# Differential attention head loop: moved taps, diagonals, rotary copies, values and layer norm's root

## The chip, the cores and the metric

One core of a Trainium2 chip runs the whole program. The metric is the device time in microseconds (us) of that core. TensorE does the matmuls, VectorE, ScalarE and GpSimd work on tiles of 128 partitions, and the sync engine's queue issues the weights' DMAs. Each engine runs its own list of instructions in order, and waits on semaphores for the others.

## The reference, cut to what matters

The program computes two transformer blocks over 512 tokens of width 1024 in float32. The change lies in the mixer of the second block, which joins differential attention with a convolution:

```python
def hybrid_mixer(h, positions, ...):
    q, k, v, u = split(h @ w_in)                 # 4 heads; q and k have 2 components of 64, v has 128
    q, k = partial_rope(q), partial_rope(k)
    # causal; for each head and component:
    p = softmax(q @ k.T / sqrt(64))
    a = p[0] - lam * p[1]                        # lam is one scalar
    a = rmsnorm(a @ v, subln_g) * (1 - lam_init) # over a head's 128 values
    c = u[..., :512] * sigmoid(u[..., 512:])
    c = causal_dwconv(c, cv_dw_w) + cv_dw_b      # 31 taps
    c = silu(layernorm(c, cv_ln_g, cv_ln_b))
    return concat(a, c) @ w_out
```

Cross attention over 256 memory rows follows, and its keys and values (`m @ w_ckv`) don't depend on the mixer, so they are computed in between.

## The kernel before, in words

Activations are held feature by feature: a tile is 128 features by 512 tokens. To keep float32 accuracy in matmuls, each operand is split into a high part (suffix `H`, written by ScalarE's copy) and a low part (suffix `L`, what remains, made by VectorE's `low`), and a product takes three matmuls (`three`, L468 to L470). Weights come in pieces of 128 x 512: a DMA to one of 4 `raw` buffers, then a split by GpSimd (L2557, L2559) to one of 7 slots, which comes free when TensorE has used the piece.

All order is written out by hand, once for each engine: the functions `pe`, `act`, `dve`, `pool` and `sync` hold the same named steps, each in its own engine's order, and `wait_ge(engine, event)` and `did(event)` connect them. There is no planner. PSUM has eight banks. `take` pops the first bank of a list and waits until its last reader is done, and `give` puts it at the end with the event that frees it. Two banks are kept out of this queue for a time: that of the convolution by VectorE (`acc_bank`) and that of the convolution tile by TensorE (`ctap`).

The steps of the stage, for four heads `hd`, each with two projections `j = 2 hd` (q) and `2 hd + 1` (k):

- `rotary_in(j)`: TensorE projects to the bank `rt`; ScalarE copies it to `tmp[j % 2]`.
- `rotate(j)`: TensorE permutes `tmp` (L961) to the bank `rts`; VectorE multiplies by cosine and sine and adds; ScalarE makes the high half of q or k; `rotated(j)` on VectorE makes the low half (`d_qL`, `d_kL`).
- `d_scores(hd)`: for each of four query tiles `n`, TensorE makes the scores of both components (L978), and adds the mask (L981). VectorE takes the maximum (L2359), ScalarE the exponential and its sum, VectorE the inverse, and ScalarE and VectorE combine the two components in `d_P`. `between` holds work that TensorE does behind a tile.
- `d_turned(hd)`: TensorE transposes the probabilities in four tiles (L1007), split to `uH`/`uL` rows 4 to 7.
- `d_values(hd)`: values by probabilities into the bank `do`, which ScalarE squares into `sums`.
- `stat_end("dn", hd)`: TensorE sums the squares over features with a matrix of ones (L501); ScalarE's `rstd` makes the root (logarithm, then exponential); `d_normed` scales the tile and splits it.
- Convolution: of 4 tiles, VectorE does three, 31 taps each (`some_taps`), TensorE the fourth by diagonal matrices (`conv_taps`, L996) that ScalarE makes (`diagonals`), eight buffers in rotation. `convolved(i)` is ScalarE's copy out of the bank.
- Layer norm: `mu` sums four tiles (L1051), VectorE centres (`cent`), squares are summed, `stat_end("ln")` and `rstd("ln")` give the root, VectorE scales (`lnn`), ScalarE applies silu.
- `memory_keys(4)`, `memory_keys(6)` and `xvalues(0)` are the memory's keys and values; the output projection `w_out_2` opens with three output tiles at once (`three_open`, `three_step`).

Of the kernel before, what the change touches and what calls it, by code (L numbers as in the profile page):

```python
# [279 lines left out]
BY_PE = 3  # L280


def build(nc, xT, pT, memT, pos, pos2, vec, cst, ws, out):
    PLAN, BEHIND, DIVIDED = plan()
    with ExitStack() as ctx:
# [147 lines left out]
        def pe():  # L433
# [3 lines left out]
            def take(*event):  # L437

                b = banks.pop(0)
                if b.freed:  # L440
                    P.wait_ge(*b.freed)
                bank_of[event] = b.ap
                return b
# [514 lines left out]
            def rotate(j):  # L958
                b = take("rts", j)
# [51 lines left out]
            def d_values(hd):  # L1011
# [9 lines left out]
                give(b, V, "y2L", hd)  # L1021
# [17 lines left out]
            for hd in range(2):  # L1039
# [4 lines left out]
                rotate(2 * hd + 5)  # L1044
                conv_taps(20 + 8 * hd, min(24 + 8 * hd, 31))
                d_values(hd)
                stat_end("dn", hd, tiles=1, tail=False)
            b = take("mu")
# [6 lines left out]
            d_turned(2)  # L1055
            d_scores(3, {1: lambda: memory_keys(4)})
            memory_keys(6)
            stat_end("ln", tiles=4, tail=False, freed=(V, "lnn", 3))
            d_values(2)
            stat_end("dn", 2, tiles=1, tail=False)  # L1060
            d_turned(3)
            xvalues(0)
            d_values(3)
            stat_end("dn", 3, tiles=1, tail=False)
# [6 lines left out]
            for k in (0, 1, 2, 4, 5, 6, 7, 3):  # L1071
                three_step(lin, k, uH, uL, y2_ready, last=3)
            three_give(lin, *[(V, "h wo", o) for o in range(3)])
# [108 lines left out]
        def root(*sid):  # L1182

            if sid[0] in ("mix", "mlp", "ple", "hs", "cq", "ckv", "ln"):
                return bk("stat", *sid)[:, :]
            return tab[1][0][:, 0:256] if sid == ("mem",) else rs[:, :]
# [3 lines left out]
        def act():  # L1190
# [397 lines left out]
            def rotary_in(j):  # L1588
                A.wait_ge(P, "rt", j)
                if j > 1:  # L1590
# [9 lines left out]
            def d_scores(hd):  # L1600
# [5 lines left out]
                for n in range(4):  # L1606
# [9 lines left out]
                    if n:  # L1616
                        divide(n - 1)
                divide(3)
# [13 lines left out]
            def d_normed(hd):  # L1632
                A.wait_ge(V, "dn", hd)
                do(uH[:, hd, :], bk("do", hd)[:, :], ACT.Copy).then_inc(*A.did("y2H", hd))
# [23 lines left out]
            d_scores(0)  # L1658
            diagonals(12, 16)
            rotary_in(2)  # L1660
# [4 lines left out]
            for hd in range(2):  # L1665
                d_turned(hd)
                d_scores(hd + 1)
                diagonals(20 + 8 * hd, 28 + 8 * hd)
                rotary_in(2 * hd + 4)
                rotary_in(2 * hd + 5)  # L1670
                rotate(2 * hd + 4)
                rotate(2 * hd + 5)
                d_values(hd)
                rstd(128, "dn", hd)
                d_normed(hd)
            convolved(2)
            for i in range(4):
                A.wait_ge(V, "cent", i)
                square(("ln",), i, d_acc[:, i, :])
            d_turned(2)  # L1680
            d_scores(3)
            memory_keys(4)
            memory_keys(6)
            rstd(512, "ln")
            d_values(2)
            rstd(128, "dn", 2)
            d_normed(2)
            d_turned(3)
# [102 lines left out]
        def dve():  # L1791
# [529 lines left out]

            def rotate(j):
                t, y = tmp[j % 2][:, :], bk("rt", j)[:, :]
                s = 1.0 if j % 2 else 0.125
                V.wait_ge(A, "rt", j)
                V.wait_ge(V, "turn")
                stt(y, y, s, C[:, :], MUL, MUL).then_inc(*V.did("rc", j))
                V.wait_ge(P, "rts", j)
                stt(t, bk("rts", j)[:, :], s, Sn[:, :], MUL, MUL).then_inc(*V.did("rts", j))
                V.wait_ge(V, "rts", j)  # L2330
                tt(y, y, t, ADD).then_inc(*V.did("rr", j))
# [7 lines left out]
            def d_scores(hd):  # L2339
# [12 lines left out]
                for n in range(4):  # L2352
# [9 lines left out]
                    if n:  # L2362
                        combine(n - 1)
                combine(3)
# [24 lines left out]

            rotate(0)  # L2390
            rotate(1)
# [4 lines left out]
            d_scores(0)  # L2396
            some_taps(2)
            rotate(2)
            rotate(3)
            rotated(2)  # L2400
            some_taps(1)
            rotated(3)
            for hd in range(2):
# [290 lines left out]
```

## Time and profile before

| | |
|---|---|
| median of 3 runs | 2405.92 us (2403.82 to 2407.05) |
| the profiled execution | 2401.89 us, span 2400.0 us |
| TensorE busy | 2298.3 us, 96% of the span |
| VectorE, ScalarE, GpSimd busy | 53%, 27%, 65% |
| mean granted clock of TensorE | 0.988 |

The profile is of one execution. The span runs from its first to its last instruction, and the profiled execution's own time, 2401.89 us, contains it. Times of a row are measured from the span's start. The stage of this change lies between about 1689 and 1850 us.

### The profile page before, as it was taken

How to read it: one execution, taken by the hardware profiler on the slowest of the kernel's cores; microseconds unless marked ns; L12 is line 12 of the kernel's file. 1: busy time of each engine (PE TensorE's matmuls, PEld its weight loads, DVE VectorE, ACT ScalarE, POOL GpSimd, SP SyncE). 2: the span in 40 equal slices, each digit the busy share in tenths (PEclk: the TensorE clock that was granted, in tenths of full speed). 3: DMA queues.
4: the chain of work that ended last, by engine and by line, in shares of the span. 5: the costliest groups of instructions: out<-in, count | busy, mean ns of one | idle time of the engine just before them, and what ended most of it. 6: DMA issues, size and time to landing. Idle time of an engine off the chain costs nothing.

```text
span 2400.0 us, 27442 instructions
## 1 busy us (share of the span) xinstructions
PE 2298.3 (96%) x10372; PEld 1860.2 (78%) x10372; DVE 1269.0 (53%) x1820; ACT 648.8 (27%) x1190; POOL 1563.6 (65%) x1530
## 2 busy tenths in 40 slices
PE   8999989999998899999999999999988999999998
PEld 6888877888887577778778888778647787888886
DVE  6674726235346666165454364468763443635444
ACT  3443432101014355154221011141444232202112
POOL 7556557877775454554597777598315946878784
PEclk9999999999999899999999999999998999999999
DMA  5222222333332111211233333233112422333332
GB/s 163 77 71 82 68 80 83 107 99 98 97 92 75 53 39 37 70 40 45 75 117 105 99 110 101 79 101 106 48 31 71 113 63 79 97 98 96 99 95 75
DMA packets 110867, 200.13 MB, mean 83 GB/s; under 512 B 12304, under 2 KB 18704, under 8 KB 110736
## 3 DMA queue, kind: packets, MB, share of 16 engines
q1 hardware_dynamic: 107568, 194.72, 27.0%
q10 hardware_dynamic: 3168, 3.67, 0.5%
q8 instruction: 82, 1.34, 0.2%
q14 instruction: 49, 0.40, 0.0%
HBM read 196.24 MB, written 2.10 MB: 83 GB/s over the span
## 4 chain that ended last, share of the span: by engine, by line
PE 87%; DVE 7%; ACT 2%; POOL 2%; issue 1%; DMA 0%; SPq 0%; DVEq 0%; POOLq 0%; ACTq 0%
PE bank L468 26%; PE bank L470 26%; PE bank L469 26%; DVE bank L1801 2%; DVE h L1793 1%; POOL wL L2559 1%; PE bank L501 1%; PE bank L996 1%; POOL wH L2557 1%; PE bank L862 1%; PE bank L867 1%; PE bank L868 1%; PE bank L863 1%; PE bank L864 1%; DVE aL L1801 1%
## 5 line engine op out<-in xcount | busy, mean ns | idle before, releaser
L2559 POOL TENSOR_TENSOR wL<-raw,wH 128x512 fp32r<-128x512 f32 (+2 forms) x731 | 997.9, 1365 | 60.9
L2557 POOL TENSOR_SCALAR wH<-raw 128x512 fp32r<-128x512 f32 (+2 forms) x731 | 528.9, 724 | 650.3 <-PE bank L470 558.4
L468 PE MATMUL bank<-aH,wH 128*128 128x512 f32 x1376 | 546.1, 397 | 18.1 <-DVE aL L1801 8.8
L470 PE MATMUL bank<-aH,wL 128*128 128x512 f32 x1376 | 537.6, 391 | 0.0
L469 PE MATMUL bank<-aL,wH 128*128 128x512 f32 x1376 | 537.1, 390 | 0.0
L468 PE MATMUL bank<-uH,wH 128*128 128x512 f32 x960 | 375.5, 391 | 5.6 <-DVE uL L1793 5.6
L469 PE MATMUL bank<-uL,wH 128*128 128x512 f32 x960 | 374.4, 390 | 0.0
L470 PE MATMUL bank<-uH,wL 128*128 128x512 f32 x960 | 374.3, 390 | 0.0
L468 PEld LDWEIGHTS bank<-aH,wH 128*128 128x128 f32 x1376 | 258.8, 188 | 77.8 <-issue 12.4
L469 PEld LDWEIGHTS bank<-aL,wH 128*128 128x128 f32 x1376 | 259.0, 188 | 56.3 <-issue 3.7
L470 PEld LDWEIGHTS bank<-aH,wL 128*128 128x128 f32 x1376 | 258.7, 188 | 54.9
L468 PEld LDWEIGHTS bank<-uH,wH 128*128 128x128 f32 x960 | 180.8, 188 | 44.6 <-ACT uH L1205 6.4
L469 PEld LDWEIGHTS bank<-uL,wH 128*128 128x128 f32 x960 | 180.8, 188 | 37.9 <-issue 0.5
L470 PEld LDWEIGHTS bank<-uH,wL 128*128 128x128 f32 x960 | 180.7, 188 | 37.8
L1205 ACT ACTIVATE uH<-mr 128x512 fp32r<-128x512 f32 x64 | 40.5, 633 | 391.0 <-DVE mr L1801 391.0
L1793 DVE TENSOR_TENSOR F<-F,bank 128x512 f32<-128x512 f32 x56 | 38.5, 687 | 190.0 <-PE bank L470 190.0
L1801 DVE SCALAR_TENSOR_TENSOR mr<-bank,rs 128x512 f32<-128x512 f32 x64 | 44.0, 688 | 157.9 <-PE bank L470 142.0
L1801 DVE SCALAR_TENSOR_TENSOR bank<-F,vs,bank 128x512 f32<-128x512 f32 x138 | 103.8, 752 | 34.9 <-ACT bank L1205 23.8
L1793 DVE TENSOR_TENSOR h<-h,bank 128x512 f32<-128x512 f32 x88 | 60.4, 686 | 112.4 <-PE bank L470 110.8
L1793 DVE TENSOR_TENSOR sums<-sums,sq 128x512 f32<-128x512 f32 (+1 forms) x72 | 78.3, 1088 | 76.5 <-ACT sq L1205 76.4
L2566 POOL TENSOR_SCALAR m_P<-m_P,m_stat 128x512 f32<-128x512 f32 x64 | 44.7, 698 | 102.0 <-DVE m_stat L2217 100.0
L1801 DVE SCALAR_TENSOR_TENSOR c_cb<-c_xb,vs,c_cb 128x511 f32<-128x511 f32 x88 | 82.4, 937 | 40.3 <-ACT c_cb L1205 38.7
(306 smaller groups left out, 3209.7 us busy)
## 6 DMA issues: line engine op xcount, KB each, us to landing
raw<-in_ws SPq DMA_DIRECT2D x699, 256.0 KB, 2.6
raw<-in_ws SPq DMA_DIRECT2D x24, 192.0 KB, 2.3
h<-in_xT SPq DMA_DIRECT2D x4, 512.0 KB, 6.6
E<-in_memT ACTq DMA_DIRECT2D x16, 128.0 KB, 2.5
out<-c_F SPq DMA_DIRECT2D x8, 256.0 KB, 2.1
tmp<-in_pT ACTq DMA_DIRECT2D x4, 256.0 KB, 3.6
raw<-in_ws SPq DMA_DIRECT2D x8, 128.0 KB, 2.0
g_hc<-in_cst SPq DMA_DIRECT2D x1, 640.0 KB, 9.2
```

Source lines behind the costliest of these rows:

```text
L468: P.e.matmul(o, lH, rH, start=start, stop=False, skip_group_check=skip)
L469: P.e.matmul(o, lH, rL, start=False, stop=False, skip_group_check=skip)
L470: return P.e.matmul(o, lL, rH, start=False, stop=stop, skip_group_check=skip)
L501: i = P.e.matmul(b.ap[:, 0:n], ones, sums[:, 0:n], start=True, stop=not tail)
L862: P.e.matmul(b.ap[:, :], m_qnH[:, c], m_knH[:, :], start=True, stop=False)
L863: P.e.matmul(b.ap[:, :], m_qnH[:, c], m_knL[:, :], start=False, stop=False)
L1205: return A.e.activation(o, i, func, bias=bias, scale=scale)
L1793: return V.e.tensor_tensor(o, a, b, op)
L1801: return V.e.scalar_tensor_tensor(o, a, s, b, op0, op1)
L2557: G.e.tensor_scalar(H, x, 1.0, 0.0, MUL, ADD).then_inc(*G.did("wH", n))
L2559: G.e.tensor_tensor(L, x, H.bitcast(F32), SUB).then_inc(*G.did("w", n))
L2566: G.e.tensor_scalar(x, x, m_st[:, 4 * (hd % 2) + n, 2:3], 0.0, MUL, ADD).then_inc(*G.did("mP", hd, n))
```

## The change

In the order of the engines:

- TensorE: `take` may take the second bank of the queue. In the head loop `d_values(hd)` moves between the two rotations, the second of which takes the second bank; three taps stand between it and the statistic, and in the first pass one behind it. The `do` bank is freed by the normed tile (`dn`). `d_turned(2)` goes ahead of `mu`; the layer norm's statistic reads `sq` and its bank is freed by ScalarE's logarithm; `d_turned(3)` goes ahead of the statistic of head 2, and the statistic of head 3 behind the first step of the output projection.
- ScalarE: `d_scores` gets `between` too: diagonals and the first rotary copy go between query tiles 2 and 3, the third convolved tile too; the transposed probabilities go ahead of `d_normed`; the layer norm's squares go to four buffers in head 3's scores.
- VectorE: the product with cosine gets its own step (`turned_by_cos`); taps go between query tiles; the normed tile is written to `tmp[0]` instead of its bank; the layer norm's root is in the SBUF tile `C`; its squares are added by `add_ln_squares` in head 3's scores.

```diff
@@ pe: take, rotate, d_values, head loop
-            def take(*event):
-                b = banks.pop(0)
+            def take(*event, second=False):
+                b = banks.pop(1 if second else 0)
...
-            def rotate(j):
-                b = take("rts", j)
+            def rotate(j, second=False):
+                b = take("rts", j, second=second)
...
-                give(b, V, "y2L", hd)
+                give(b, V, "dn", hd)
...
                 rotary_in(2 * hd + 5)
                 rotate(2 * hd + 4)
-                rotate(2 * hd + 5)
-                conv_taps(20 + 8 * hd, min(24 + 8 * hd, 31))
                 d_values(hd)
+                rotate(2 * hd + 5, second=True)
+                conv_taps(20 + 8 * hd, 23 + 8 * hd)
                 stat_end("dn", hd, tiles=1, tail=False)
+                if hd == 0:
+                    conv_taps(23, 24)
+            d_turned(2)
             b = take("mu")
...
-            d_turned(2)
             d_scores(3, {1: lambda: memory_keys(4)})
             memory_keys(6)
-            stat_end("ln", tiles=4, tail=False, freed=(V, "lnn", 3))
+            b = take("stat", "ln")
+            P.wait_ge(V, "sum", ("ln",))
+            P.e.matmul(b.ap[:, :], ones, sq[:, :], start=True, stop=True).then_inc(*P.did("stat", "ln"))
+            give(b, A, "ln", "ln")
             d_values(2)
+            d_turned(3)
             stat_end("dn", 2, tiles=1, tail=False)
-            d_turned(3)
             xvalues(0)
             d_values(3)
-            stat_end("dn", 3, tiles=1, tail=False)
...
                 three_step(lin, k, uH, uL, y2_ready, last=3)
+                if k == 0:
+                    stat_end("dn", 3, tiles=1, tail=False)
@@ root
-            return tab[1][0][:, 0:256] if sid == ("mem",) else rs[:, :]
+            return tab[1][0][:, 0:256] if sid == ("mem",) else C[:, :] if sid == ("ln",) else rs[:, :]
@@ act
-                if j > 1:
+                if j in (4, 6):
+                    A.wait_ge(V, *(("y2L", 0) if j == 6 else ("rr", 2)))
+                elif j > 1:
                     A.wait_ge(V, "rr", j - 2)
...
-            d_scores(0)
-            diagonals(12, 16)
-            rotary_in(2)
+            d_scores(0, {2: lambda: (diagonals(12, 16), rotary_in(2))})
...
-                d_turned(hd)
-                d_scores(hd + 1)
-                diagonals(20 + 8 * hd, 28 + 8 * hd)
-                rotary_in(2 * hd + 4)
+                if hd == 0:
+                    d_turned(0)
+                d_scores(hd + 1, {2: lambda: (convolved(2) if hd else None, diagonals(20 + 8 * hd, 28 + 8 * hd), rotary_in(2 * hd + 4))})
                 rotary_in(2 * hd + 5)
                 rotate(2 * hd + 4)
+                d_values(hd)
                 rotate(2 * hd + 5)
-                d_values(hd)
                 rstd(128, "dn", hd)
+                d_turned(hd + 1)
                 d_normed(hd)
-            convolved(2)
-            for i in range(4):
-                A.wait_ge(V, "cent", i)
-                square(("ln",), i, d_acc[:, i, :])
-            d_turned(2)
-            d_scores(3)
+            def squares():
+                for i, x in enumerate((sq, tmp[1], C, Sn)):
+                    A.wait_ge(V, "cent", i)
+                    do(x[:, :], d_acc[:, i, :], ACT.Square).then_inc(*A.did("sq", ("ln",), i))
+            d_scores(3, {1: squares})
...
+            d_values(2)
             rstd(512, "ln")
-            d_values(2)
+            d_turned(3)
             rstd(128, "dn", 2)
             d_normed(2)
-            d_turned(3)
@@ dve
+            def turned_by_cos(j):
+                y = bk("rt", j)[:, :]
+                V.wait_ge(A, "rt", j)
+                V.wait_ge(V, "turn")
+                stt(y, y, 1.0 if j % 2 else 0.125, C[:, :], MUL, MUL).then_inc(*V.did("rc", j))
...
             def d_normed(hd):
-                y = bk("do", hd)[:, :]
+                y = tmp[0][:, :]
                 V.wait_ge(A, "rstd", "dn", hd)
-                stt(y, y, lam[:, 5:6], root("dn", hd), MUL, MUL).then_inc(*V.did("dn", hd))
+                V.wait_ge(V, *(("rr", 2 * hd + 4) if hd < 2 else ("y2L", hd - 1)))
+                stt(y, bk("do", hd)[:, :], lam[:, 5:6], root("dn", hd), MUL, MUL).then_inc(*V.did("dn", hd))
...
-                d_turned(hd)
-                d_scores(hd + 1)
-                some_taps(6)
+                d_scores(hd + 1, {2: lambda: some_taps(4)} if hd == 0 else {1: lambda: some_taps(200)})
+                turned_by_cos(2 * hd + 4)
+                some_taps(1)
                 rotate(2 * hd + 4)
+                turned_by_cos(2 * hd + 5)
+                rotated(2 * hd + 4)
                 rotate(2 * hd + 5)
-                rotated(2 * hd + 4)
-                some_taps(1)
                 rotated(2 * hd + 5)
+                if hd:
+                    V.wait_ge(P, "ctap")
+                    ts(d_acc[:, BY_PE, :], bk("ctap")[:, :], vv("cv_dw_b_2", BY_PE), None, ADD, None).then_inc(*V.did("conv", BY_PE))
                 d_normed(hd)
+                d_turned(hd + 1)
...
-            for i in range(1, 4):
-                add_squares(("ln",), i)
-            d_turned(2)
-            d_scores(3)
+            def add_ln_squares():
+                x = (sq, tmp[1], C, Sn)
+                for i in (0, 2):
+                    V.wait_ge(A, "sq", ("ln",), i + 1)
+                    tt(x[i][:, :], x[i][:, :], x[i + 1][:, :], ADD).then_inc(*V.did("sum2", ("ln",), i))
+                V.wait_ge(V, "sum2", ("ln",), 2)
+                tt(sq[:, :], sq[:, :], C[:, :], ADD).then_inc(*V.did("sum", ("ln",)))
+            d_scores(3, {1: add_ln_squares})
             memory_keys(4)
             memory_keys(6)
-            d_normed(2)
...
             d_turned(3)
+            d_normed(2)
```

## Rows read from the trace of the kernel before

**Rows 1.** Table by stretch: span, busy us (x instructions), clock, DMA, GB/s.

```profile
core 0: us, PE busy (x) PEld busy (x) DVE busy (x) ACT busy (x) POOL busy (x), PEclk, DMA share, GB/s
1689.40:1850.00 160.60, 139.22 (x620) 95.06 (x619) 93.34 (x187) 69.97 (x171) 55.72 (x59) 0.95 0.16 48
...
1762.20:1765.50 3.30, 3.30 (x6) 1.23 (x5) 2.97 (x8) 1.86 (x8) 0.00 (x0) 0.50 0.02 5
1799.70:1806.40 6.70, 4.36 (x20) 4.36 (x21) 4.37 (x13) 3.95 (x14) 1.18 (x2) 0.50 0.00 1
1827.00:1833.70 6.70, 4.84 (x12) 3.82 (x13) 3.36 (x7) 3.52 (x5) 1.69 (x2) 0.50 0.01 2
```

**Rows 2.** Waits of TensorE, 1683 to 1850: total us, times, longest.

```profile
PE bank L978 <- DVE uL L1793: 3.3, 3, 2.6
...
PE bank L501 <- ACT sums L1205: 2.9, 4, 0.8
PE bank L961 <- ACT tmp L1205: 2.3, 3, 1.7
PE bank L468 <- DVE d_qL L1793: 2.2, 2, 1.6
PE bank L1051 <- ACT F L1205: 1.6, 1, 1.6
```

**Rows 3.** Timeline of TensorE: start, us, instruction, [idle before <-releaser].

```profile
1745.46 1.96 PE L961 MATMUL bank<-tmp,cs 128*128 128x512 f32 x4 [1.67 <-ACT tmp L1205]
1747.26 3.60 PE L996 MATMUL bank<-F,sq 128*128 128x512 f32 x8
1752.46 0.50 PE L468 MATMUL bank<-uH,d_VH 128*128 128x512 f32 x1 [1.61 <-DVE d_qL L1793]
...
1755.27 1.13 PE L501 MATMUL bank<-sums,cs 128*128 128x512 f32 x2 [0.69 <-ACT sums L1205]
...
1756.23 1.25 PE L1007 MATMUL bank<-cs,F 128*128 128x128 f32 x10
1760.06 0.33 PE L978 MATMUL bank<-d_kH,d_qH 64*128 64x128 f32 x2 [2.57 <-DVE uL L1793]
...
1761.21 0.39 PE L978 MATMUL bank<-d_kH,d_qH 64*128 64x256 f32 x2 [0.23 <-DVE uL L1793]
...
1762.04 5.34 PE L996 MATMUL bank<-F 128*128 128x512 f32 x8
...
1802.04 0.58 PE L468 MATMUL bank<-x_mH,wH 128*128 128x256 f32 x1 [3.05 <-DVE uL L1793]
...
1809.85 0.45 PE L978 MATMUL bank<-d_kH,d_qH 64*128 64x384 f32 x2
...
1828.86 0.77 PE L468 MATMUL bank<-wH,x_mH 128*128 128x512 f32 x1 [5.24 <-DVE F L1801]
...
1845.19 1.10 PE L501 MATMUL bank<-sums,cs 128*128 128x512 f32 x2 [0.78 <-ACT sums L1205]
```

**Rows 4.** Timeline of ScalarE, same columns.

```profile
1744.74 1.06 ACT L1205 ACTIVATE tmp<-bank 128x512 f32<-128x512 f32 x2
...
1758.61 1.75 ACT L1205 ACTIVATE uH<-bank 128x512 fp32r<-128x512 f32 x4 [0.83 <-DVE bank L1801]
```

**Rows 5.** Timeline of VectorE, same columns.

```profile
1738.21 1.29 DVE L2359 TENSOR_REDUCE d_stat<-bank 128x1 f32<-128x512 f32 x2 [3.71 <-PE bank L981]
...
1757.82 0.76 DVE L1801 SCALAR_TENSOR_TENSOR bank<-bank,lam,rs 128x512 f32<-128x512 f32 x1 [4.16 <-ACT rs L1205]
...
1845.59 2.09 DVE L1793 TENSOR_TENSOR uL<-F,uH 128x512 fp32r<-128x512 f32 x2 [15.24 <-ACT uH L1205]
...
1850.59 0.69 DVE L1793 TENSOR_TENSOR uL<-bank,uH 128x512 fp32r<-128x512 f32 x1 [0.84 <-ACT uH L1205]
```

**Rows 6.** Timeline of GpSimd, same columns: one weight piece and the next's start.

```profile
1807.29 0.62 POOL L2557 TENSOR_SCALAR wH<-raw 128x512 fp32r<-128x512 f32 x1 [0.16 <-PE bank L470]
1807.99 1.29 POOL L2559 TENSOR_TENSOR wL<-raw,wH 128x512 fp32r<-128x512 f32 x1
1809.24 0.62 POOL L2557 TENSOR_SCALAR wH<-raw 128x512 fp32r<-128x512 f32 x1
```

More of the change, by code:

```diff
@@ L1182, in root @@
         def root(*sid):
-            if sid[0] in ("mix", "mlp", "ple", "hs", "cq", "ckv", "ln"):
+            if sid[0] in ("mix", "mlp", "ple", "hs", "cq", "ckv"):
                 return bk("stat", *sid)[:, :]
-            return tab[1][0][:, 0:256] if sid == ("mem",) else rs[:, :]
+            return tab[1][0][:, 0:256] if sid == ("mem",) else C[:, :] if sid == ("ln",) else rs[:, :]
         def act():
@@ L1598, in rotate, with d_scores @@
                 do(d_qk[2 * (j % 2)][:, :], bk("rt", j)[:, :], ACT.Copy).then_inc(*A.did("rH", j))
-            def d_scores(hd):
+            def d_scores(hd, between={}):
                 def divide(n):
@@ L1617, in d_scores @@
                         divide(n - 1)
+                    if n in between:
+                        between[n]()
                 divide(3)
@@ L1633, in d_normed @@
                 A.wait_ge(V, "dn", hd)
-                do(uH[:, hd, :], bk("do", hd)[:, :], ACT.Copy).then_inc(*A.did("y2H", hd))
+                do(uH[:, hd, :], tmp[0][:, :], ACT.Copy).then_inc(*A.did("y2H", hd))
             def convolved(i):
@@ L2324, in rotate @@
                 s = 1.0 if j % 2 else 0.125
-                V.wait_ge(A, "rt", j)
-                V.wait_ge(V, "turn")
-                stt(y, y, s, C[:, :], MUL, MUL).then_inc(*V.did("rc", j))
                 V.wait_ge(P, "rts", j)
@@ L2330, in rotate @@
                 V.wait_ge(V, "rts", j)
+                V.wait_ge(V, "rc", j)
                 tt(y, y, t, ADD).then_inc(*V.did("rr", j))
@@ L2337, in rotated, with d_scores @@
                 low(L[:, :], bk("rt", j)[:, :], H[:, :]).then_inc(*V.did("rL", j))
-            def d_scores(hd):
+            def d_scores(hd, between={}):
                 def combine(n):
@@ L2363, in d_scores @@
                         combine(n - 1)
+                    if n in between:
+                        between[n]()
                 combine(3)
@@ L2388, in xvalues @@
                     low(d_VL[:, 2 * t + half, :], bk("xV", half, t)[:, :], d_VH[:, 2 * t + half, :]).then_inc(*V.did("xVL", half, t))
+            turned_by_cos(0)
             rotate(0)
+            turned_by_cos(1)
             rotate(1)
@@ L2395, in dve @@
             some_taps(3)
-            d_scores(0)
-            some_taps(2)
+            d_scores(0, {2: lambda: some_taps(4)})
+            turned_by_cos(2)
             rotate(2)
+            turned_by_cos(3)
             rotate(3)
             rotated(2)
-            some_taps(1)
             rotated(3)
+            d_turned(0)
             for hd in range(2):
-                d_turned(hd)
-                d_scores(hd + 1)
-                some_taps(6)
+                d_scores(hd + 1, {2: lambda: some_taps(4)} if hd == 0 else {1: lambda: some_taps(200)})
+                turned_by_cos(2 * hd + 4)
+                some_taps(1)
                 rotate(2 * hd + 4)
+                turned_by_cos(2 * hd + 5)
+                rotated(2 * hd + 4)
                 rotate(2 * hd + 5)
-                rotated(2 * hd + 4)
-                some_taps(1)
                 rotated(2 * hd + 5)
+                if hd:
+                    V.wait_ge(P, "ctap")
+                    ts(d_acc[:, BY_PE, :], bk("ctap")[:, :], vv("cv_dw_b_2", BY_PE), None, ADD, None).then_inc(*V.did("conv", BY_PE))
                 d_normed(hd)
-            some_taps(200)
-            V.wait_ge(P, "ctap")
-            ts(d_acc[:, BY_PE, :], bk("ctap")[:, :], vv("cv_dw_b_2", BY_PE), None, ADD, None).then_inc(*V.did("conv", BY_PE))
+                d_turned(hd + 1)
             V.wait_ge(P, "mu")
```

## The prediction, made blind

> **What bounds the kernel now.** I began with the page's first part: TensorE is busy for 96% of the span (table above), so only its idle or slowed time can be won. The table by stretch then gives the total for the diff's stage: from 1689.4 to 1850.0 it is busy 139.22 of 160.60 us, so 21.4 us are idle, and three stretches have its granted clock at 0.50, the lower of its levels (1.2 GHz) [rows 1]. The waits of that window show for whom it stands: VectorE and ScalarE, never the weights [rows 2]. The timelines show each gap and the engines that end it [rows 3 to 6].
>
> A low clock costs only while there is work. Behind the gap of 1760 eight tap matmuls took 5.34 us instead of 3.60 [rows 3]: 1.7 us lost. In the second stretch work begins at 1802.04 and the low clock ends near 1806.4: half of 4.4, 2.2 us. In the third it is half of 1828.86 to 1833.8, 2.5 us. Together 6.4 us. All three stretches come with a gap of 2.57, 3.05 or 5.24 us [rows 1, 3]; smaller gaps had none. The Trainium skill (TensorE: Matmul & The Clock Gate, Part 1) says that the throttled state is the default and activity releases it; the rows agree.
>
> **What costs nothing.** The diff adds no matmul and leaves the weights' order and DMAs alone. TensorE's work in the stage is therefore constant, and the sum is idle and low clock before, less what is left of both.
>
> **Part 1: taps, diagonals and the first rotary copy between score tiles 2 and 3.** Before, ScalarE copies the first rotary tile behind the head's scores and eight diagonals, at 1744.74 [rows 4]; the rotation at 1745.46 had waited 1.67 us [rows 3]. Now the copy follows its projection, about 1737. Queued behind this wait on ScalarE are tile 3's exponentials; they need maxima of scores that come later still, at 1738.21, so nobody waits. VectorE idles for 3.71 us until then [rows 5]; four taps at about 0.75, 3.0 us, go into it (3.0 us more if that cover were gone). The waits at the rotations, L961, 2.3 us in three [rows 2], go.
>
> **Part 2: values between two rotations.** VectorE's chain of products, sum and low half behind the rotations kept the values waiting, 2.2 us in two heads [rows 2], because their bank was the one that the low half of q frees. Now they take a bank that a score tile freed long before, and the rotation behind them takes the second in the queue, free too. Squaring the values, which kept the statistic waiting 0.69 us [rows 3], lies under the rotation and three taps, 0.9 + 2.7 us (two matmuls of 0.45 to a tap, from 3.60 for eight [rows 3]). Both go in both heads.
>
> **Part 3: normed tile in SBUF, and the stalls that come.** Call S the start of a head's statistic. Before, S is 1755.27, the normed tile is done at 1758.58 (S + 3.31) and ScalarE turns to its high half at 1758.61; the next head's second score tile starts at 1761.21 (S + 5.94) [rows 3 to 5]. Counting banks in queue order, the fourth transposed tile now waits for the values' bank, free at S + 3.31. In the loop's first pass TensorE has before it the statistic 0.96, a tap 0.90 and nine of ten transposes, 1.12 (1.25 for ten [rows 3]): S + 3.0, a wait of 0.4. ScalarE now takes the probabilities' high halves first and starts that of the normed tile near S + 4.0, 0.65 later; on VectorE the probabilities' low halves are queued behind the normed tile's, and the second score tile waits for two of them, to S + 6.6. Between, TensorE has one score tile, 0.92 us (1761.21 - 0.23 - 1760.06 [rows 3]): it stands 2.1 us. I keep the 1.7 us of low clock here, for this is the place and kind of the gap that brought it before. In the second pass no tap stands behind the statistic: the fourth transposed tile waits from S + 2.1 to S + 3.4, 1.3 us; then the mean's eight matmuls, 3.6 us, reach beyond S + 6.6. The wait at head 1's second score tile stays, 0.5 us (what L978's 3.3 us leave beside 2.57 and 0.23 [rows 2, 3]).
>
> **Part 4: layer norm.** Its third convolved tile is copied during head 2's scores, so the mean no longer waits: L1051, 1.6 us [rows 2]. Centring, some 2.5 us of VectorE, used to stand before the low halves for which the memory keys waited 3.05 us at 1802.04 [rows 3]; those are now done ahead. Two score tiles 1.8, the keys 5.6 (1802.04 to 1809.85 less 2.2 [rows 3]) and tile 2, 1.1, put its scores some 5.9 us behind the centring's end. Exponentials, four squares at 0.6 and one addition end 5.4 to 6.5 us behind it. A lateness of 0.6 there has about 1 us of room before the last head's transposes need the last probability tile. I take 0; the bound is 1 us of waiting.
>
> **Part 5: root in SBUF, last heads.** Before, the statistic's bank came free with the fourth scaled tile, and the memory values waited 5.24 us for it at 1828.86 [rows 3]. Now it is free when ScalarE has read it, ahead of the transposes' end. The last two statistics go behind transposes and behind the first output step, so their part of L501's 2.9 us in four waits [rows 2] goes like that of the first two. The last probabilities are needed only behind the memory values, 11 us (1828.86 to 1844.4, less 2.5 of low clock and 2 of values [rows 3]).
>
> A price comes with it: a subtraction with both inputs in SBUF took 1.05 us (2.09 for two) beside GpSimd's work, one that read a bank 0.69 [rows 5]. Three low halves, four scalings and an addition become such: 8 x 0.4 = 3.2 us of VectorE. They lie under the memory values, but for those of the first passes, when GpSimd rests. I take 0 on the path, 3.2 as the bound. The Trainium skill (SBUF — State Buffer, Who interferes with whom) says that such an instruction contends with GpSimd's reads and that the first to start blocks the other. The 1.05 us agrees; by the rule the gain is at most 3.2 us less, and GpSimd loses as much.
>
> **Weights.** A piece costs GpSimd 0.62 + 1.29, by its starts 1.97 us [rows 6]; keys and memory values use one in 1.4 (5.6 for four). Seven lie ready when the keys start, at T. A slot is free again when its piece was used, so the last memory-value piece is ready 3.4 us behind the first one's use and needed 9.6 behind it; the first output piece at 5.4, needed at 12.7. No wait.
>
> **The sum.** Idle 21.4, low clock 6.4. A gap is counted from a modelled end that overlaps the next start (the statistic ends at 1756.40, the next matmul starts at 1756.23 [rows 3]), so each of twelve gaps gives another 0.16: 1.9. Left: 0.5 + 0.4 + 2.1 + 1.3 idle and 1.7 low clock, 6.0. Gain 21.4 + 6.4 + 1.9 - 6.0 = **23.7 us**. Work behind 1850 is TensorE's own and follows. The profiled execution took 2401.89 us (span 2400.0): it becomes 2378.2. The runs' median lies 4.0 above it, so **2382 us**. Bounds: no low clock, 1.7 more gain; the waits of 1 us and 3.2 us on the path and one more low stretch of 1.7, 5.9 less. Own range 2380 to 2388.
>
> **Rivals.**
> - *The chain moves rather than goes.* My 2.1 and 1.3 us come from the new orders on ScalarE and VectorE; further ones may. If both bring a second low stretch (2 x 1.7), the last transposes wait 2 us with another (3.7) and SBUF operands cost 3.2, the gain is 23.7 - 10.3 = 13.4: 2392.5. Against it: most covers exceed 1 us. Chance 0.17.
> - *No low clock and shorter new stalls.* The wait of 2.1 halves, low clock goes: 23.7 + 2.8: 2379. Chance 0.2.
> - *No change.* If taps overran their 3.71 us by several, each maximum, exponential and rotation in three heads would follow late, and 3 x 7 us would be back: 2403. The rows give a 3.0 us load. Chance 0.04.
> - *Slower.* Earlier demand finds GpSimd late. Fifteen pieces behind the seven are needed by T + 37; to lose 29 us there, past the gain and 5 more, 1.4 + 15c must exceed 66, so c over 4.3 us instead of 1.97. At 4.5 it is 1.4 + 67.5 - 37 = 32 us late: 2414. Contention adds under 1 us a piece. Chance 0.03.
>
> The forecast itself has 0.56. About 0.2% (5 us) is what a measurement of this kernel can tell from no change: the first three cases are faster, 0.93; same 0.04; slower 0.03. The range reaches from the second rival less 2 to the first: 2377 to 2393.
>
> **What would show it.** No wait at the rotations nor at the values; the statistic near 1749 in the first pass and 1781 in the second; about 2 us of wait at head 2's second score tile, 1.3 at its fourth transposed tile; none before memory keys or memory values; the first output step near 1821.5 instead of 1846. It is wrong if the copy between tiles delays tile 3's exponentials, if the last head's tile 2 is late by more than a few us, or if TensorE waits for weights.

## The result, and the profile after

| | before | after |
|---|---|---|
| median | 2406.34 us | 2379.01 us (2378.41 to 2379.91) |
| ratio | | 0.9889, 95% interval 0.9871 to 0.9906 |
| profiled execution, its span | 2401.89, 2400.0 us | 2379.13, 2376.9 us |
| the stage, first rotation to a fixed matmul | 163.59 us | 137.85 us |

The change makes the kernel 27.3 us faster by the medians. Of 30 further executions of the kernel before, six took 2400.6 to 2401.9 us at a mean granted clock of 0.987 or 0.988 and 24 took 2403.9 to 2408.1 at 0.985 to 0.987, so the profiled one, 2401.89 at 0.988, belongs with the six. The last line of the table compares the same work in both traces: from the first rotation's matmul to the same output projection matmul (in each trace the 632nd behind it; the order between them changed, the set did not). In the trace of before it is 1853.41 - 1689.82, after it is 1830.38 - 1692.53:

```profile
1853.41 0.39 PE L470 MATMUL bank<-uH,wL 128*128 128x512 f32 x1
```

```profile
1692.53 0.59 PE L961 MATMUL bank<-tmp,cs 128*128 128x512 f32 x1
...
1830.38 0.39 PE L470 MATMUL bank<-uH,wL 128*128 128x512 f32 x1
```

So the stage gives 25.7 us. The spans differ by 23.1 only, because the stage starts 2.7 us later in the trace after, and the diff has no part in that: 1.2 us of it stand already at the first matmul (9.97 against 8.82), and most of the rest comes with a low-clock stretch near 1613 that the trace of before doesn't have. The table by stretch (columns as in [rows 1]) has it below the stage's line:

```profile
core 0: us, PE busy (x) PEld busy (x) DVE busy (x) ACT busy (x) POOL busy (x), PEclk, DMA share, GB/s
1689.40:1826.60 137.20, 132.98 (x631) 92.72 (x630) 97.37 (x190) 67.55 (x166) 58.07 (x60) 1.00 0.19 56
1613.30:1616.70 3.40, 3.09 (x7) 2.48 (x8) 3.37 (x5) 2.26 (x4) 3.32 (x4) 0.50 0.22 78
```

The reader is to see three things in the stage's line. TensorE is idle for 4.2 of 137.2 us, where it was 21.4 of 160.6 [rows 1]. Its granted clock is 1.00 throughout, where it was 0.95. And what went was waiting, not work: over the same work, from the first rotation to the fixed matmul, VectorE is busy for 95.7 us in both traces and ScalarE for 71.4 before and 71.3 after. (The rows above and in [rows 1] have round bounds and don't hold quite the same instructions.) The wait view of TensorE for the stage answers to [rows 2]; of eight entries two are left:

```profile
PE bank L978 <- DVE uL L1804: 2.6, 2, 2.0
PE bank L1007 <- DVE tmp L1812: 1.6, 2, 1.2
```

TensorE's timeline, answering to [rows 3], has them one by one:

```profile
1727.93 0.39 PE L978 MATMUL bank<-d_kH,d_qH 64*128 64x256 f32 x2 [0.60 <-DVE uL L1804]
...
1745.61 1.02 PE L961 MATMUL bank<-tmp,cs 128*128 128x512 f32 x2
1748.34 1.07 PE L961 MATMUL bank<-tmp,cs 128*128 128x512 f32 x2
...
1751.82 1.02 PE L501 MATMUL bank<-sums,cs 128*128 128x512 f32 x2
...
1755.07 0.33 PE L1007 MATMUL bank<-cs,F 128*128 128x128 f32 x1 [0.39 <-DVE tmp L1812]
...
1758.24 0.39 PE L978 MATMUL bank<-d_kH,d_qH 64*128 64x256 f32 x2 [1.99 <-DVE uL L1804]
...
1782.13 1.02 PE L501 MATMUL bank<-sums,cs 128*128 128x512 f32 x2
...
1785.37 0.33 PE L1007 MATMUL bank<-cs,F 128*128 128x128 f32 x1 [1.24 <-DVE tmp L1812]
```

The two rotations stand apart now, with the values between them and no wait at either. Behind the statistic of 1751.82 stand the two stalls that the prediction placed there. The timelines of ScalarE and VectorE say why the second score tile has to wait until 1758.24:

```profile
1754.18 1.54 ACT L1211 ACTIVATE uH<-bank 128x512 fp32r<-128x512 f32 x4
1755.61 0.62 ACT L1211 ACTIVATE uH<-tmp 128x512 fp32r<-128x512 f32 x1
```

```profile
1754.27 0.75 DVE L1812 SCALAR_TENSOR_TENSOR tmp<-bank,lam,rs 128x512 f32<-128x512 f32 x1 [1.97 <-ACT rs L1211]
1756.34 0.69 DVE L1804 TENSOR_TENSOR uL<-tmp,uH 128x512 fp32r<-128x512 f32 x1 [1.32 <-ACT uH L1211]
1756.95 1.68 DVE L1804 TENSOR_TENSOR uL<-bank,uH 128x512 fp32r<-128x512 f32 x4
```

ScalarE has the probabilities' first high half well before 1755.61, but VectorE stands idle for 1.32 us with the normed tile's low half at the head of its queue, and the probabilities' low halves, which free the banks, come behind it.

### The profile page after: what moved, and what is told of

Same layout as the page of the kernel before. It is cut to its first block, busy times and chain, and to the rows that moved or that the text cites. A ratio compares the mean times of both kernels' runs of the same rounds, so it can differ in the third digit from the quotient of the medians.

```text
span 2376.9 us, 27442 instructions
## 1 busy us (share of the span) xinstructions
PE 2291.5 (96%) x10372; PEld 1857.1 (78%) x10372; DVE 1270.3 (53%) x1820; ACT 648.7 (27%) x1190; POOL 1566.0 (66%) x1530
## 4 chain that ended last, share of the span: by engine, by line
PE 89%; DVE 6%; ACT 2%; POOL 2%; issue 1%; DMA 0%; SPq 0%; DVEq 0%; POOLq 0%
PE bank L468 26%; PE bank L470 26%; PE bank L469 26%; DVE h L1804 1%; DVE bank L1812 1%; POOL wL L2587 1%; PE bank L996 1%; POOL wH L2585 1%; PE bank L501 1%; PE bank L862 1%; PE bank L867 1%; PE bank L868 1%; PE bank L863 1%; PE bank L864 1%; DVE aL L1812 1%
```

## The experiments

Twelve runs in three sets, each set timed beside the kernel before. "Stage" is the length defined above, from each run's one profiled execution; the change itself, profiled twice, has 137.85 and 137.89 us. The medians are of all executions of a run, so they also hold what happens outside the stage. "By the medians" below is against 2379.63, that of a0_change.

| run | median us | its before | stage us | against the change's 137.85 |
|---|---|---|---|---|
| a0_change | 2379.63 | 2405.74 | 137.89 | 0.0 |
| e_low_first | 2377.19 | 2405.74 | 135.87 | -2.0 |
| e_stat_first | 2376.91 | 2405.74 | 135.13 | -2.7 |
| e_norm_in_bank | 2380.55 | 2405.74 | 140.38 | +2.5 |
| u1_copy_behind | 2385.88 | 2406.20 | 143.98 | +6.1 |
| u2_values_behind | 2383.22 | 2406.20 | 141.83 | +4.0 |
| u4_squares_before | 2382.53 | 2406.20 | 142.45 | +4.6 |
| u5_root_in_bank | 2384.58 | 2406.20 | 143.58 | +5.7 |
| p5_root_alone | 2398.63 | 2406.13 | 155.83 | (before: -7.8) |
| p1_copy_alone | 2399.12 | 2406.13 | 158.83 | (before: -4.8) |
| p2_values_alone | 2399.22 | 2406.13 | 158.35 | (before: -5.2) |
| v_mixed | 2375.45 | 2406.13 | 134.81 | -3.0 |

**a0_change**, the change again, without an edit.

> The change itself again, to have it beside the variants. Theory (waits and low clock of TensorE in the stage, each part by itself): 2379 us, gain 25 to 28 over before, waits left in the stage of about 0.6, 0.4, 2.0 and 1.2 us. Rival (the gain leans on where the low-clock stretches happen to fall): a gain that differs by over 3 us from the first measurement's 27.

Ratio 0.9892 (0.9875 to 0.9908), the same four waits within 0.01 us, and no low clock in the stage. The gain by the medians is 26.1 us, 1.2 less than in the first measurement and far from the rival's 3. The stage's gain repeats to 0.04 us. What the medians give beyond it does vary: the executions of before alone spread over 7.5 us.

**e_low_first.** VectorE, both passes:

```diff
-                d_normed(hd)
-                d_turned(hd + 1)
+                d_normed(hd, lambda: d_turned(hd + 1))   # called between the scaling and the low half
```

> VectorE makes the low halves of the probabilities ahead of that of the normed tile. Theory (the 1.99 us wait at head 2's second score tile is the queue on VectorE behind the high half of the normed tile): that wait falls below 0.3 us, the statistic to second score tile from 6.4 to about 4.6 us; 2.0 us faster than the change, about 2377. Rival (the wait is for ScalarE's copies of the probabilities, late themselves): the wait stays above 1.2 us and the time within 0.8 us of the change.

The wait is gone. VectorE's timeline in this run:

```profile
1755.80 0.75 DVE L1812 SCALAR_TENSOR_TENSOR tmp<-bank,lam,rs 128x512 f32<-128x512 f32 x1 [1.97 <-ACT rs L1211]
1756.46 1.67 DVE L1804 TENSOR_TENSOR uL<-bank,uH 128x512 fp32r<-128x512 f32 x4
1758.05 0.68 DVE L1804 TENSOR_TENSOR uL<-tmp,uH 128x512 fp32r<-128x512 f32 x1
```

The 1.32 us of idle time no longer stand ahead of the low halves, and TensorE's second score tile (head 2's) starts 4.4 us behind the statistic (1757.76 against 1753.35), not 6.4. Stage 2.0 us shorter, as expected to the tenth. It was VectorE's queue, and not ScalarE's copies.

**e_stat_first.** The same, and on TensorE:

```diff
-                conv_taps(20 + 8 * hd, 23 + 8 * hd)
                 stat_end("dn", hd, tiles=1, tail=False)
-                if hd == 0:
-                    conv_taps(23, 24)
+                conv_taps(20 + 8 * hd, min(24 + 8 * hd, 31))
```

> As the run before, and all taps of TensorE stand behind the statistic instead of before it, in both passes; VectorE finishes the tap tile behind the normed tile. Theory (waits in TensorE's order: the chain of root and normed tile needs 3.3 us of cover, and squaring needs only the rotation's 0.9): the waits of 0.39 and 1.24 us at the fourth transposed tiles go too, none above 0.3 us left but the 0.6 of head 1; 3.6 us faster than the change, about 2375.5. Rival (VectorE's and ScalarE's chain of the k rotation sets the statistic's root anyway): the statistic starts earlier but the normed tile does not, and the gain over the change stays at 2 us.

In the second pass the theory is right: the 1.24 us went and only 0.17 came. In the first neither is. The statistic starts earlier, at 1749.10 (1751.82 in the change, whose stage starts 0.5 us later). ScalarE's timeline has the k rotation's high half ahead of the root in the queue, and that waits for VectorE's sum, so part of this is lost; the root still starts at 1750.92 instead of 1752.88, and the normed tile comes 1.5 us earlier within the stage.

```profile
1750.43 0.60 ACT L1209 ACTIVATE d_kH<-bank 128x512 fp32r<-128x512 f32 x1 [1.69 <-DVE bank L1802]
1750.92 0.68 ACT L1209 ACTIVATE rs<-bank,cs 128x512 f32<-128x512 f32 x1
...
1754.14 1.43 ACT L1209 ACTIVATE uH<-bank 128x512 fp32r<-128x512 f32 x4 [1.87 <-PE bank L1007]
```

But nothing waits for the normed tile any more. All four taps now stand between statistic and transposes, the transposes come 0.4 us later within the stage, ScalarE idles 1.87 us for them, and the second score tile waits 0.46 us for the low halves. Stage 0.7 us less than with low halves first, where 1.6 was expected.

**e_norm_in_bank.** Part 3 undone:

```diff
-                give(b, V, "dn", hd)
+                give(b, V, "y2L", hd)
...
-                d_turned(hd + 1)
                 d_normed(hd)
+                d_turned(hd + 1)
...
-                y = tmp[0][:, :]
+                y = bk("do", hd)[:, :]
```

> Part 3 undone: normed tile written to its bank, the bank free with its low half, ScalarE writes the high half of the normed tile before those of the probabilities. Theory: fourth transposed tile of head 1 waits from S + 3.0 to S + 4.75 (1.7 us), second score tile of head 2 then at S + 5.9, without a wait, 0.5 us earlier than in the change; in the second pass the fourth transposed tile waits 2.6 us instead of 1.24. Sum 0.9 us slower than the change, 2380. Rival (the tile in SBUF carries a large part of the gain, since its bank came free late): 3 us or more slower, 2382 or above.

```profile
PE bank L1007 <- DVE uL L1804: 4.5, 2, 2.7
PE bank L978 <- DVE uL L1804: 0.6, 1, 0.6
```

The two waits at the fourth transposed tile are 1.82 and 2.68 us (expected 1.7 and 2.6), and the second score tile has none. In idle time that is 0.9 more than in the change; the median is 0.9 up too. The profiled execution also had one low-clock stretch behind the 2.68 us wait, 1.7 us of the 2.5 by which its stage is longer. The three edits of part 3 (the tile's place, the earlier release of its bank and the order of the copies) are together worth about 1 us without that stretch. That the order gives back much of what the tile's place gains is argued from e_low_first's 2.0 us; no run undoes the one without the other.

**u1_copy_behind.** Part 1 undone:

```diff
-            d_scores(0, {2: lambda: (diagonals(12, 16), rotary_in(2))})
+            d_scores(0)
+            diagonals(12, 16)
+            rotary_in(2)
...
-                d_scores(hd + 1, {2: lambda: (convolved(2) if hd else None, diagonals(20 + 8 * hd, 28 + 8 * hd), rotary_in(2 * hd + 4))})
+                d_scores(hd + 1, {2: lambda: convolved(2) if hd else None})
+                diagonals(20 + 8 * hd, 28 + 8 * hd)
+                rotary_in(2 * hd + 4)
```

and VectorE's `{2: lambda: some_taps(4)}` likewise behind the scores of heads 0 and 1.

> Part 1 undone in the change: taps, diagonals and the first rotary copy behind the head's scores, on VectorE and ScalarE. Theory (three separate waits at the rotations, 0.5, 1.7 and 0.15 us): they come back in that size, the statistic starts later by no more than that; 2.3 to 3 us slower than the change, 4.5 with a low-clock stretch: 2381.5 to 2383.5. Rival (VectorE's four taps are the point: each on the chain of the rotations, 3 us in each of two heads): over 6 us slower, 2385 or more.

```profile
PE bank L978 <- DVE uL L1808: 2.8, 2, 2.0
PE bank L961 <- ACT tmp L1211: 2.3, 3, 1.7
PE bank L1007 <- DVE tmp L1816: 1.6, 2, 1.2
PE bank L1007 <- DVE d_qL L1808: 1.2, 1, 1.2
```

The three waits for copies are back at just 2.3 us, but a fourth that I had not seen comes with them: 1.2 us at head 0's first transposed tile, for the bank that the low half of head 1's q frees, late by VectorE's four taps. And the low clock is back (0.50 from 1764.1 to 1767.3, TensorE busy throughout), under taps, 1.7 us. Sum 2.3 + 1.2 + 0.2 at a score tile + 1.7 + some 0.5 of overlaps = 5.9, measured 6.1 (6.2 by the medians). The time is the rival's, over twice the theory's 2.3 to 3 and above its 4.5 with a low-clock stretch. The rival named VectorE's taps rightly, but they cost 1.2 us in one head, not 3 in each of two.

**u2_values_behind.** Part 2 undone:

```diff
-                d_values(hd)
-                rotate(2 * hd + 5, second=True)
-                conv_taps(20 + 8 * hd, 23 + 8 * hd)
-                stat_end("dn", hd, tiles=1, tail=False)
-                if hd == 0:
-                    conv_taps(23, 24)
+                rotate(2 * hd + 5)
+                conv_taps(20 + 8 * hd, min(24 + 8 * hd, 31))
+                d_values(hd)
+                stat_end("dn", hd, tiles=1, tail=False)
```

and ScalarE's square behind the k high half.

> Part 2 undone in the change: both rotations, taps, then values, then the statistic. Theory: the values no longer wait for q's low half, because that is now done by 1749.5 and the values come at 1751; but the statistic waits 0.7 to 1 us for the squares, and the fourth transposed tile 1.2 us in both passes instead of 0.4 and 1.2. 2.8 us slower than the change in all, 2382. Rival (the values' wait of 1.6 and 0.6 us of before comes back as well): 5 us or more slower, 2384 or more.

```profile
PE bank L978 <- DVE uL L1802: 2.7, 2, 2.1
PE bank L501 <- ACT sums L1209: 1.4, 2, 0.7
PE bank L978 <- DVE tmp L1810: 1.1, 1, 1.1
PE bank L1007 <- DVE x_kL L1802: 0.8, 1, 0.8
```

No wait at the values, 0.69 us for squares in each pass, as the theory has it: with the rest of the change in place, q's low half is early enough for the values in their old place too. The queue of banks shifts, so the 1.1 us wait for the normed tile is at head 2's first score tile, and only in the first pass. A wait of 0.84 us for the memory keys' low half appears at the last head's transposes. One low-clock stretch, 1.7 us, makes the rest: 4.0 in the stage, 3.6 by the medians, expected 2.8.

**u4_squares_before.** Part 4 undone, but for the early copy of the convolved tile:

```diff
-            d_turned(2)
             b = take("mu")
...
+            d_turned(2)
             d_scores(3, {1: lambda: memory_keys(4)})
...
-            d_scores(3, {1: squares})
+            for i in range(4):
+                A.wait_ge(V, "cent", i)
+                square(("ln",), i, d_acc[:, i, :])
+            d_turned(2)
+            d_scores(3)
```

and the same order on VectorE, its sums one by one.

> Part 4 undone in the change: the mean ahead of head 2's transposes, the layer norm's squares one by one and their sums before the last head's scores, VectorE's low halves of head 2 behind them. The convolved tile stays early. Theory: the memory keys wait about 3 us again, and with it comes a low-clock stretch that costs about 2 us more; the 1.24 us wait at the fourth transposed tile goes in return. 4 us slower, 2383 (2 with no low clock). Rival (later work absorbs it, because the keys are needed late): within 1 us of the change.

The wait at the memory keys is 3.05 us, the very figure of before [rows 3], with a low-clock stretch over it:

```profile
1790.80:1797.50 6.70, 4.35 (x20) 4.35 (x21) 4.38 (x13) 3.95 (x14) 1.18 (x2) 0.50 0.00 1
```

TensorE was busy for 4.35 of these 6.7 us, so it lost 2.2. The 1.24 us wait went in return, one of 0.7 came. Stage 4.6 us longer, 2.9 by the medians, 4 expected. The edit moves transposes, centring and squares together, so the run doesn't tell them apart.

**u5_root_in_bank.** Part 5's root undone:

```diff
-            if sid[0] in ("mix", "mlp", "ple", "hs", "cq", "ckv"):
+            if sid[0] in ("mix", "mlp", "ple", "hs", "cq", "ckv", "ln"):
...
-            give(b, A, "ln", "ln")
+            give(b, V, "lnn", 3)
```

> Part 5's root undone in the change: layer norm's root in its bank, free with the fourth scaled tile; the order of transposes and statistics stays as in the change. Theory (the 5.24 us wait was the bank, but the scaling now starts earlier against TensorE): the memory values wait from 1809.2 to about 1812, 2.7 us, with low clock up to 1.7 us more; 2.7 to 4.5 us slower, 2382 to 2383.5. Scaled tiles 2.7 us for four instead of 3.1. Rival (the whole of the old wait and its low clock, 5.2 + 2.5, hang on this tile): 7 us or more slower, 2386.

```profile
1810.73 0.77 PE L468 MATMUL bank<-wH,x_mH 128*128 128x512 f32 x1 [2.69 <-DVE F L1812]
```

```profile
1807.91 2.72 DVE L1812 SCALAR_TENSOR_TENSOR F<-F,vs,bank 128x512 f32<-128x512 f32 x4 [1.87 <-ACT bank L1211]
```

```profile
1810.20:1816.80 6.60, 6.07 (x14) 4.79 (x15) 3.37 (x7) 4.10 (x7) 2.74 (x3) 0.50 0.01 2
```

The wait ends with the fourth scaled tile and is 2.69 us, as expected. The low clock behind it is the larger cost: it holds for twice the length that I allowed, and TensorE is busy for 6.07 us of it, so 3.0 are lost. 2.7 + 0.2 + 3.0 = 5.9; measured 5.7 in the stage and 5.0 by the medians, between the theory's 4.5 and the rival's 7.

Why 2.69 us here and 5.24 before, for the same bank? The traces point to the queue on VectorE, whose order no run changed by itself. TensorE has the layer norm's statistic at 1803.19 in this run, and the scaled tiles start 4.7 us later, ahead of head 2's normed tile. Before, the statistic stood at 1817.78 and the scaled tiles came 8.3 us later, behind the normed tile's low half:

```profile
1817.78 1.02 PE L501 MATMUL bank<-sums,cs 128*128 128x512 f32 x2
```

```profile
1825.44 0.69 DVE L1793 TENSOR_TENSOR uL<-bank,uH 128x512 fp32r<-128x512 f32 x1 [0.73 <-ACT uH L1205]
1826.05 2.71 DVE L1801 SCALAR_TENSOR_TENSOR F<-F,vs,bank 128x512 f32<-128x512 f32 x4
```

**p5_root_alone, p1_copy_alone, p2_values_alone.** The same edits the other way round, each alone, put into the kernel before. The copy's run leaves the product with cosine where it was, the values' run leaves the normed tile in its bank. For the root:

```diff
-            if sid[0] in ("mix", "mlp", "ple", "hs", "cq", "ckv", "ln"):
+            if sid[0] in ("mix", "mlp", "ple", "hs", "cq", "ckv"):
...
-            return tab[1][0][:, 0:256] if sid == ("mem",) else rs[:, :]
+            return tab[1][0][:, 0:256] if sid == ("mem",) else C[:, :] if sid == ("ln",) else rs[:, :]
...
-            stat_end("ln", tiles=4, tail=False, freed=(V, "lnn", 3))
+            stat_end("ln", tiles=4, tail=False)
```

> Part 5's root alone, put into the kernel before: layer norm's root in SBUF, its statistic's bank free with ScalarE's logarithm. Theory (in the kernel before the whole 5.24 us wait before the memory values is that bank, since the scaled tiles come late there; undone in the change it cost only 2.68 of wait): the wait goes entirely and the low clock behind it too, 5.24 + 0.16 + 2.5 = 7.9 us faster than before, 2398. Rival (another bank or operand comes as late, the last probabilities or the memory keys' low half): a wait of 2 us or more stays there, gain 5 us or less.

The wait at the memory values is gone and nothing took its place. Stage 155.83 us, 7.8 less than before, against 7.9 expected; 7.5 by the medians, against this set's before (ratio 0.9971, 0.9959 to 0.9984).

> Part 1 alone, put into the kernel before (taps, diagonals and first rotary copy between score tiles; product with cosine left where it was). Theory (undoing it in the change returned 2.3 us of wait for copies and about 1.2 to 1.4 us at banks that VectorE's rotation frees): the waits for copies go, that of the values shrinks from 1.61 to about 0.4 us, that at head 2's first score tile stays 2.6: 4 us faster than before, 2402. Rival (the statistic's chain behind takes it up, as a wait that another step ends): waits for copies go, the wait at head 2's first score tile grows by as much, gain under 1.5 us.

Stage 4.8 us less than before, 7.0 by the medians, 4 expected (ratio 0.9976, 0.9965 to 0.9987); the waits for copies went, that of the values went wholly in the first pass and is 0.44 in the second, and head 2's first score tile still waits 2.57: the rival's take-up did not happen.

```profile
PE bank L978 <- DVE uL L1791: 3.4, 3, 2.6
...
PE bank L468 <- DVE d_qL L1791: 0.4, 1, 0.4
```

> Part 2 alone, put into the kernel before (values between the rotations, one tap behind the statistic; normed tile still in its bank, free with its low half). Theory: values' waits (2.2 us) and the statistic's two first waits (1.4) go; the fourth transposed tile waits about 1.7 us for the values' bank, in exchange for part of the 2.57; head 2's second score tile comes 5.9 us behind the statistic as before. The statistic comes 3.5 us earlier in the first pass and 1.6 in the second: 5 us faster than before, 2401. Rival (the values between the rotations delay the k rotation, on which scores wait): a new wait for k's low half of over 1 us, gain under 2.5 us.

Stage 5.2 us less, 6.9 by the medians, 5 expected (ratio 0.997, 0.996 to 0.9981). The fourth transposed tile waits 1.8 us as expected, the 2.57 us wait behind it is gone, and the low-clock stretch that followed it before (1.7 us) did not come, so that belongs to the 5.2. The rival's wait for k's low half did not come either; the statistic waits 0.56 us for a bank that q's low half frees.

```profile
PE bank L1007 <- DVE uL L1795: 1.8, 1, 1.8
...
PE bank L501 <- DVE d_qL L1795: 0.6, 1, 0.6
```

**v_mixed**, from what the two orders of taps had shown: low halves first; in the first pass the change's taps, in the second the statistic ahead of all three.

```diff
-                conv_taps(20 + 8 * hd, 23 + 8 * hd)
+                if hd == 0:
+                    conv_taps(20, 23)
                 stat_end("dn", hd, tiles=1, tail=False)
-                if hd == 0:
-                    conv_taps(23, 24)
+                conv_taps(*((28, 31) if hd else (23, 24)))
```

> The change with the low halves of the probabilities first, the first pass as there (three taps, statistic, one tap), the second with the statistic ahead of all three taps. Theory (each pass needs 3.3 us of cover behind its statistic; in the first the k rotation's chain on ScalarE sets the root, so nothing is won by going earlier): waits of 0.6, 0.39 and 0.2 us, 0.7 us less than with low halves first alone; stage 3.2 us shorter than in the change, about 2376. Rival (the order of taps is of no use in either pass): the wait of 1.24 us stays in another place, time as with low halves first, 2377.

```profile
PE bank L978 <- DVE uL L1804: 0.6, 1, 0.6
PE bank L1007 <- DVE tmp L1812: 0.4, 1, 0.4
PE bank L501 <- DVE d_qL L1804: 0.2, 1, 0.2
```

Waits 0.6, 0.4 and 0.2, as expected; stage 134.81 us, 3.0 less than the change (3.2 expected) and 1.1 less than low halves first alone (0.7 expected), but only 0.3 less than e_stat_first. Its executions lie between 2374.4 and 2375.67 us, those of the change, in two sets, between 2378.41 and 2379.91: it beats both kernels (ratio to before 0.9872, 0.9858 to 0.9887).

## Why the prediction was right, and where it was off

- **The sum.** I predicted 23.7 us; the stage gives 25.7. The terms hold: idle 21.4 before and 4.2 after, 6.4 of low clock gone, 1.9 for twelve gaps, together 25.5. The waits left were put at 0.5, 0.4, 2.1 and 1.3; they are 0.60, 0.39, 1.99 and 1.24. The term that was mis-sized is the low clock of "1.7 us" that I kept behind the 2.1 us stall: no low clock came in the stage, measured twice. That is 1.7 of the 2.0 us between sum and stage.
- **The median.** The forecast, 2382, is 3 us above the measured 2379.01, which lies below my own range (2380 to 2388) and inside the wide one (2377 to 2393). Three things made it up. The stage gave 2.0 more than the sum. The stage started 2.7 us later in the trace after, so that the profiled execution, forecast at 2378.2, took 2379.13; that the two nearly cancel is luck. And I carried over the 4.0 us between the profiled execution and the median of before, which is 0 after (2379.13 and 2379.01). Where before's usual executions lose their 4 us isn't shown, for they were not profiled; their lower mean granted clock (0.985 or 0.986 for most, 0.988 in the profiled one) points to low clock. So the stage's 25.7 us are shown, and what the medians give on top of them is not explained.
- **Part 1.** Mechanism shown from both sides: copies 2.3 us. Its cover held: VectorE's four taps took 3.12 us and left 0.67 us of idle time before tile 3's maximum (0.7 foreseen). Not in the prediction was that the copy and the taps also bring VectorE's low halves forward: undone it costs 1.2 us at head 0's first transposed tile, alone it takes the values' wait along. So the part is worth 4.8 us alone, with a low-clock stretch up to 6.1, where the 2.3 us row made it look like the smallest.
- **Part 2.** The statistic's waits go, shown from both sides (0.69 us in each pass come back when undone). The values' waits (2.2 us) go by this part alone, but most of them (1.8) go by part 1 alone too, and undone in the change none comes back: either part takes them, so they can't be booked to one. 5.2 us alone, 4.0 undone.
- **Part 3.** The stalls were placed and sized rightly, and e_low_first shows their cause. By itself the part gives 0.9 us (e_norm_in_bank).
- **Part 4.** Shown for transposes, centring and squares together: 3.05 us of wait and 2.2 of low clock come back when undone. The early convolved tile and the later statistics were not undone; that they give the 1.6 us and the rest of L501's waits is read from the traces alone. The thin place at the last transposes held with no wait in the change, and u2_values_behind shows how thin: 0.84 us there.
- **Part 5.** Shown: 7.8 us alone. The same edit undone in the change is 5.7, with 2.69 of wait instead of 5.24, since there VectorE scales the layer norm's tiles ahead of the normed tile. The prediction looked only at the bank; by the traces the new order on VectorE, which no run undid by itself, takes about half of the wait too. Single parts alone (7.8, 4.8, 5.2) and undone (5.7, 6.1, 4.0, 4.6) are two different cuts through one sum: neither is the part's share of the 25.7.
- **SBUF operands.** The price was put at 3.2 us of VectorE as a bound, 0.4 for each of eight instructions. Four scalings took 3.10 us in the change and 2.72 with the root in its bank, 0.4 in all. Beside GpSimd's work one addition took 1.35 and one 0.98; the first took 0.69:

```profile
1794.97 0.69 DVE L1804 TENSOR_TENSOR sq<-sq,tmp 128x512 f32<-128x512 f32 x1 [0.61 <-ACT tmp L1211]
1796.01 1.35 DVE L1804 TENSOR_TENSOR C<-C,Sn 128x512 f32<-128x512 f32 x1 [0.35 <-ACT Sn L1211]
1797.40 0.98 DVE L1804 TENSOR_TENSOR sq<-sq,C 128x512 f32<-128x512 f32 x1
```

  The low halves of the normed tile took 0.69 us each, no more than from a bank. So some 1.3 of the 3.2 us came, and GpSimd's busy time in the stage rose from 55.7 to 58.0 us for the same 58 instructions. None of it reached TensorE, as assumed.
- **Weights.** No wait for them; GpSimd's slots were the ones that waited (1.52 us for TensorE at 1810.83).
- **The rivals.** No low clock came, as the second rival had it, and its time, 2379, is the measured one; but its new stalls did not shrink: 1.7 of its 2.8 us came as it said, and the rest of its number is met by the 4.0 us above. The three others did not happen.

## What to carry to other kernels

In a stage where one engine's work is constant and its order is written out, list that engine's gaps with the low clock behind them, then count the banks in queue order for the new program: the new stalls were found, and sized to about 0.1 us, by that count and a chain measured once (statistic to normed tile, 3.31 us). Look at what stands at the head of each helper engine's queue while it idles: low halves that free banks belong ahead of one that waits for a tile nobody needs yet. And judge an edit by the bank's last reader rather than by its arithmetic, for one root moved out of a bank was worth 7.8 us in the kernel before. Two edits can remove the same wait, so try each alone and each undone before you book a gain to one.

## What the hardware did that I had not expected

The same wait brought the low clock in one run and not in another. After 1.99 us at head 2's second score tile the clock stayed at 1.00 in the change, both times, and in u4_squares_before and u5_root_in_bank, and fell to 0.50 in u1_copy_behind; behind 2.07 us, with 1.13 shortly before, it fell in u2_values_behind; behind waits of 2.57 to 5.24 us it fell in every trace taken, at 2.68 us in e_norm_in_bank for a stretch that cost 1.7 us and at 2.69 us in u5_root_in_bank for one that cost 3.0. So a wait of some 2 us costs itself or nearly double, and one of 2.7 us cost up to 5.7. The stretches before the stage vary between executions of the same work as well: that near 1613 stands in 12 of the 14 traces, and not in those of the kernel before and of p5_root_alone.
